# The order in which three PSUM banks of a head go back into the queue of free banks

## What is computed

```python
p = h @ w_in                                   # 1024 x 6672
qkv, z, beta_r, a_r, hq, hf_fwd, hf_bwd, hi, hgate, gate_dn, gate_hg = split(p)
q, k, v = heads(silu(dwconv(qkv)))             # 4 heads of 128, q and k to unit norm
o_dn = gated_delta(q, k, v, beta[0], g[0]) + flip(gated_delta(flip(q), ..., g[1]))
ih = heads(hi)                                 # the values of the second scan
o_hg = hgrn2(qh, kk[0], ih, logf[0]) + flip(hgrn2(flip(qh), kk[1], flip(ih), logf[1]))
merged = sigmoid(gate_dn) * (norm(o_dn, z) @ w_branch_dn) \
       + sigmoid(gate_hg) * (norm(o_hg, hgate) @ w_branch_hg)
return merged @ w_out
```

## Time and profile before

| | |
|---|---|
| median of 3 runs | 1540.56 us (1540.35 to 1541.1) |
| the profiled execution | 1539.32 us, span 1537.5 us |
| TensorE, matmuls | 1510.3 us busy, 98% of the span |
| TensorE, weight loads | 1404.9 us, 91% |
| DVE | 1202.3 us, 78% |
| ACT | 1015.8 us, 66% |
| granted TensorE clock, mean | 0.996 |
| read from HBM | 242.58 MB, 158 GB/s over the span |

### The profile page before, as it was taken

How to read it: one execution, slowest core, us unless ns; L and a number is a source line. 1 busy time by engine, 2 the same in 40 slices (tenths; PEclk the granted TensorE clock), 3 DMA queues, 4 the chain that set the end, 5 groups by cost and what they waited for, 6 DMA issues and landing times.

```text
span 1537.5 us, 29846 instructions
## 1 busy us (share of the span) xinstructions
PE 1510.3 (98%) x12702; PEld 1404.9 (91%) x12702; DVE 1202.3 (78%) x1709; ACT 1015.8 (66%) x1566; POOL 8.3 (1%) x18
## 2 busy tenths in 40 slices
PE   9999999999999999999999999999999998999998
PEld 9999999988889999999988889968999897899997
DVE  7999766889758799667898768886888578688864
ACT  7786864667647776765676546685777557677753
POOL 0000000000000000000000000000000001000000
PEclk9999999999999999999999999999999999999999
DMA  7522145555554422244655646402655543255551
GB/s 290 192 100 96 56 141 189 203 185 191 211 175 161 145 103 85 84 165 165 225 193 186 214 169 238 150 17 83 220 187 186 194 149 136 79 202 188 191 192 55
DMA packets 35700, 245.55 MB, mean 160 GB/s; under 512 B 4208, under 2 KB 4592, under 8 KB 6512
## 3 DMA queue, kind: packets, MB, share of 16 engines
q1 hardware_dynamic: 35568, 243.65, 44.4%
HBM read 242.58 MB, written 1.05 MB: 158 GB/s over the span
## 4 chain that ended last, share of the span: by engine, by line
PE 83%; DVE 10%; ACT 5%; DMA 1%; issue 1%; SPq 0%; DVEq 0%; ACTq 0%
PE PS L419 82%; DVE WL L1980 2%; DVE SA L1980 1%; ACT WH L1236 1%; ACT SB L1233 1%; DVE SB L1980 1%; DVE SB L1989 1%; PE PS L422 1%; DMA RAW<-a_w_gl 1%; DVE SB L2255 1%; DMA RAW<-w_in 1%; ACT SB L1907 1%; DVE SA L1989 0%; DVE SA L2157 0%; DVE SB L1984 0%
## 5 line engine op out<-in xcount | busy, mean ns | idle before, releaser
L419 PE MATMUL PS<-XHL,WH 128*128 128x256 f32 (+2 forms) x4080 | 848.2, 301 | 5.1 <-ACT SA L1411 2.8
L419 PEld LDWEIGHTS PS<-XHL,WH 128*128 128x128 f32 (+1 forms) x4080 | 646.2, 187 | 41.8 <-issue 6.5
L419 PE MATMUL PS<-XHL,WL 128*128 128x256 f32 (+1 forms) x2392 | 670.2, 280 | 0.0
L1236 ACT CAST WH<-RAW 128x2048 fp32r<-128x2048 f32 (+1 forms) x235 | 427.3, 1822 | 281.1 <-PE PS L419 267.4
L1980 DVE TENSOR_TENSOR WL<-RAW,WH 128x2048 fp32r<-128x2048 f32 (+1 forms) x235 | 511.8, 2181 | 113.8 <-ACT WH L1236 110.1
L419 PEld LDWEIGHTS PS<-XHL,WL 128*128 128x128 f32 (+1 forms) x2392 | 449.0, 188 | 0.4
L419 PE MATMUL PS<-INHL,WH 128*128 128x512 f32 (+1 forms) x1216 | 334.4, 344 | 1.2 <-DVE INHL L1980 1.2
L419 PE MATMUL PS<-INHL,WL 128*128 128x256 f32 x960 | 270.0, 281 | 0.0
L419 PEld LDWEIGHTS PS<-INHL,WH 128*128 128x128 f32 x1216 | 210.2, 188 | 29.2 <-ACT INHL L1236 1.5
L419 PEld LDWEIGHTS PS<-INHL,WL 128*128 128x128 f32 x960 | 181.2, 189 | 0.0
L1980 DVE TENSOR_TENSOR SB<-SB 128x512 f32<-128x512 f32 (+2 forms) x162 | 108.8, 674 | 14.5 <-ACT SB L1233 11.4
(11 more groups left out here) (156 smaller groups left out, 1438.9 us busy)
## 6 DMA issues: line engine op xcount, KB each, us to landing
RAW<-w_in SPq DMA_DIRECT2D x51, 1024.0 KB, 4.9
RAW<-w_up SPq DMA_DIRECT2D x44, 1024.0 KB, 4.8
RAW<-f_in SPq DMA_DIRECT2D x44, 1024.0 KB, 4.8
RAW<-w_down SPq DMA_DIRECT2D x22, 1024.0 KB, 4.8
RAW<-f_out SPq DMA_DIRECT2D x22, 1024.0 KB, 4.8
RAW<-a_w_in SPq DMA_DIRECT2D x10, 1024.0 KB, 5.3
RAW<-w_out SPq DMA_DIRECT2D x8, 1024.0 KB, 4.8
RAW<-w_bdn SPq DMA_DIRECT2D x4, 1024.0 KB, 4.8
```

Source lines behind the costliest of these rows:

```text
L419: return e.matmul(out, l, r, start=start, stop=stop, skip_group_check=True)
L1236: e.copy(out, x).then_inc(*A.up(*key, of=of))
```

## The change

In the loop over the heads, for heads 2 and 3, the bank of the turned values used to go into the queue ahead of the two banks of the head's products. Now it goes in behind them.

```diff
                     else:
                         tokm((st, "it", h - 2), st)
-                        ps.give(st, "it", h - 2)
                     ps.give(st, "kk", h)
                     ps.give(st, "kq", h)
+                    if h >= 2:
+                        ps.give(st, "it", h - 2)
```

## The result

The changed kernel is slower, by a little: in one session with 20 runs of each, the median is 1540.8 us (1539.67 to 1543.42) and that of the kernel before 1539.59 us (1536.12 to 1541.42). The ratio is 1.0016, with a 95% interval of 1.0010 to 1.0021, that is 2.5 us more (1.5 to 3.2). It is not the ratio of the two medians, which are 1.2 us apart; the means, 1539.17 and 1541.26, are 2.1 us apart. The profiled execution took 1541.3 us with a span of 1539.5; it was 1537.5.

A forecast was written before the change was run, and what follows sets the result against it. TensorE has work in 98% of the span, but DVE sets when `dn_y(0, 1)` and `hg(0)` start. So -2.79 + 2.79 = 0 us, forecast 1540.5 us, with 8 in 10 between 1539.0 and 1542.2.

The forecast's parts named there:

- step 5: At `dn_y(0, 1)`: DVE still releases it at 124.57; pauses become 1.84 and 1.85 us, giving back all 2.79 us.
- the sum: Whole kernel: 2.79 us won at `zproj(0, 0)` and 2.79 us given back before `dn_y(0, 1)`, net 0.
- the forecast as a whole: Would count as wrong if the granted clock read below 1 behind 125 or 580 us.
- Steps 1 to 4: Renamed banks in each mixer: pauses before `zproj(0, 0)` go, 2.79 us in all; the other takes cost 0.
- The rival on the clock: Behind the joined pause TensorE's clock falls, costing 1.4 to 1.7 us a mixer, 1542.0 to 1544.0 in all; chance 0.07.
- The full gain: Rival: DVE also comes 1.39 us earlier, so both removed pauses are won, 2.79 us, giving 1537.8; chance 0.05.
- Step 6: DVE products of head 3: running beside matmuls changes each by 0.01 us either way, taken as 0.

The follow-up runs named there:

- e3: Changed kernel, but only head 2's bank given back behind the products, head 3's as before; ratio 1.0013 to the kernel before.
- e9: Changed kernel measured once more without any edit, beside others on one chip; ratio 1.0010 to the kernel before.
- e2: Changed kernel with 7 idle matmuls ahead of the waits of `dn_y(0, 1)` in both mixers; ratio 1.0005 to the kernel before.
- e1: Changed kernel with TensorE's wait for `it_out(0)` put back ahead of `zproj(0, 0)` in both mixers; ratio 1.0002 to the kernel before.
- e4: Changed kernel with `zproj(1, 1)` moved into the joined pause and `zproj(2, 0)` moved up to its old place; ratio 1.0010 to the kernel before.
- e11: Changed kernel with DVE steps reordered to release `dn_y(0, 1)` and `hg(0)` earlier, plus `back(1, 3)` and a lower half chunk moved; ratio 1.0003 to the kernel before.

## Why the prediction was wrong

The forecast of no change failed in step 5 and with it in the sum: the work behind the joined pause was taken to last as long as before. The kernel before came out 1 us lower in the larger session and the changed one at 1540.8, so that the number 1540.5 is near by luck. The change of +0.16% is smaller than the 0.2% that the text counted as no change, but its interval, 1.0010 to 1.0021, is clear of 1. The prediction's own sign against "the forecast as a whole", a clock below 1 behind 125 or 580, came true at both places.

1. Steps 1 to 4 (six takes, and what they wait for) were right, each one. No wait for line 1412 is left, and `hg_diag` took over the bank of `("it", 0)` without a pause. The experiment on head 2 alone agrees that the bank of head 3 has no part in it.
2. Step 5 was right in where the time goes and off in its amount: 2.08 and 2.06 us for 1.84 and 1.85. The pause of 1.39 us in the earlier trace rows counts from the end of one matmul to the start of the next. But matmuls overlap: in the changed kernel the next one starts at 111.89, 0.11 us behind the start of its forerunner, at 111.78, and before the end of it at 112.05. From start to start the old pause cost 1.66 - 0.11 = 1.55 us. The stream behind it was also a little shorter (120.38 - 111.89 = 8.49 us for the 8.57), for its first two matmuls took 0.40 us where they had taken 0.47 behind the pause. Together they make `hg_diag` 1.64 us earlier against the same DVE step, and 0.45 + 1.64 = 2.09.
3. What failed is the last clause of step 5 and with it the sum: "It starts at 124.57 as before", and from there everything as before. It did start as before. But the 3.02 us of narrow matmuls behind it were taken over from the earlier trace rows at 2.4 GHz, and in 5 of the 7 profiled mixers that had them behind this pause they ran for the most part at 1.2 GHz, in 4.50 to 4.56 us. `hg(0)` came 1.1 us late in each of the five.
4. The rival on the clock named this, with its place and its direction, and had 0.07. It was set low for one row: the pause of 2.09 us before 1291.69 lies in a stretch with 1.00. One execution and one place were read as a rule. At that very place the clock fell right behind the pause in 6 of the 13 profiles, and the experiment on head 2 shows that such a pause can go either way in one and the same execution. Its second support, that only further pauses brought the clock down, overlooked the row that spoke against it: around 993 the clock was at 0.57 with TensorE busy for the whole 2.00 us, and the timeline has no pause there at all; ahead of it stand 3.65 us of matmuls that are only 32 columns wide. Whoever sees a fall without any pause should not count on a 2 us pause to be harmless. The Trainium skill ("Perfetto Trace Analysis", Matmul Optimizations) wants matmuls back to back in batches because the engine scales its power with utilization. The rule gives no length and no price, but it spoke for this rival, and the trace agrees where the clock fell: 4.50 us for 3.02.
5. Its price was 1.4 to 1.7 us a mixer; measured at `hg(0)` are 1.1. The fall lasted 3.4 us, and the 96 matmuls lost 4.50 - 3.02 = 1.48 us. The slack took 0.40 us of it and not 0.32, for it too counts from start to start: 132.13 to 135.07 without a pause is 2.94 us, 130.52 to 133.86 with it 3.34. 1.48 - 0.40 = 1.08.
6. Does the sum close? The mean clock of all 42 runs of the changed kernel and of e3 is 0.9940, that of the 95 runs of the kernel before in the three sessions of the experiments 0.9956. The difference over 1538 us, at half speed, is 0.0016 x 1538 / 0.5 = 4.9 us more at 1.2 GHz in a run, or 1.4 falls of 3.4 us, and 1.4 x 1.1 = 1.6 us. Measured are 2.5 us in the session of 20 runs, 2.0 for e3 and 1.5 for e9 (1.0016, 1.0013, 1.0010). The clock of each run is rounded to 0.001, so this closes roughly; up to 0.9 us may come from elsewhere. One such place is in the profiles: late in the mixer, at the group that starts at 176.06 and 631.79 in the kernel before and at 177.27 and 634.61 in the changed one, the first mixer is 1.08 us behind and the second 1.68 (counted from the first DVE product of head 2, 0.13 and 1.14 us later in this execution). The second mixer loses the further part where a pause of 0.26 us without a known cause stands, told of at the end. How much of it belongs to the fall is open: second mixers without a fall stand there at 71.68 (the kernel before) to 72.71 (e2), the changed one at 73.36.
7. The full gain did not come, for the reason that the prediction gave. Step 6 was right: the products of head 3 took 0.55, 0.55, 0.55 and 0.54 us in the changed kernel, all beside matmuls.

## What to carry to other kernels

A pause of TensorE that is removed ahead of another engine's bound is not removed: it joins the next one. Two short pauses can cost less than one of the same total, since here the clock fell behind the long one (2.06 to 2.19 us) in 7 of 9 mixers and behind shorter ones (up to 1.6 us) in none of 17. So before a wait is taken away, look where the time will stand afterwards, and if that place already has a pause, move the step that ends it as well (here one transpose ahead of one product), or leave the wait alone.

## What was not expected of the hardware

A pause of 2.06 to 2.19 us brought the granted clock down to 1.2 GHz behind it in 7 of 9 mixers, for 3.4 us each time, though TensorE was busy all through the fall. The same work does not get the same clock in every execution: around 990 us it fell in seven of the 13 profiles (0.83 or 0.66 over ten microseconds) and not in the other six. These six are the ones in which it fell right behind the pause of the earlier trace rows; why the two exclude each other was not tested. It is part of why runs of one kernel differ by 4 to 5 us: in the runs of the kernel before, a mean clock higher by 0.001 goes with a time shorter by 0.7 us (a straight line through each of the three sessions; correlation -0.45 to -0.56).

Throwaway matmuls can pay for themselves. 1.8 us of them in a pause kept the clock and did not make `hg(0)` later in either mixer, as DVE released it. In time this is shown less well: 1.0005 beside 1.0013 in one session, with intervals that overlap.

In the second mixer, between 595 and 606 us, single pauses of 0.2 to 1.0 us stand that no semaphore explains; the profile puts them down to "issue". They vary from execution to execution: 0.73 in the kernel filled in the first mixer, 1.02 in the one filled in both, none listed in the kernel before, e1, e4 and e11. In the three executions whose second mixer had the fall at 580 they come early, at 596 to 597, with 0.26, 0.26 and 0.33 us, and in the others only from 604 on. Whether the fall brings them there is not shown, and their cause is not known.
